# A decoder step on one core: the sample's last sums, square, norm and store laid out as four column quarters on 128 partitions

## The reference

```python
# per token row x of 1024: 8 heads x 16 chosen experts = 128 rows of each table
act = gelu(einsum('chkd,cd->chk', u_emb[eid], xc))
h   = h + einsum('chk,chkd->cd', gate * act, v_emb[eid])
y   = h * rsqrt(mean(h * h, axis=-1) + 1e-6) * g_final
```

## Time and profile before

| | us |
|---|---|
| median of 3 runs | 1046.88 |
| lowest and highest | 1045.89 and 1047.12 |
| span of the profiled execution, first to last instruction | 1044.4 |
| PE, DVE, POOL, ACT busy | 768.4, 761.5, 617.4, 410.3 |
| moved by DMA | 381.40 MB, mean 365 GB/s |

### The profile page before, as it was taken

One profiled execution on the slowest core, in us unless ns is written; L12 is line 12 of the kernel. 1 busy time (PEld: TensorE's weight loads), 2 busy tenths in 40 slices (PEclk: granted clock), 3 DMA queues, 4 the chain that ended last, 5 costly groups with the idle time before them and its releaser, 6 DMA issues.

```text
span 1044.4 us, 13759 instructions
## 1 busy us (share of the span) xinstructions
PE 768.4 (74%) x4077; PEld 379.5 (36%) x4077; DVE 761.5 (73%) x1927; ACT 410.3 (39%) x1159; POOL 617.4 (59%) x584
## 2 busy tenths in 40 slices
PE   8999996456978869777559766765875855645966
PEld 3575872112544546444113333331322422211211
DVE  1362858998877454999977699999554598999441
ACT  1153133223754752333324453732774323324221
POOL 0000257777777776666676757557475665777771
PEclk9999998886987989998767968987687888886899
DMA  9924699999999999999999999999899999999994
GB/s 363 317 106 178 219 331 399 410 404 345 369 397 400 351 410 404 415 407 376 374 375 382 394 406 389 366 392 394 310 407 419 415 415 411 409 402 343 408 410 186
DMA packets 122109, 381.40 MB, mean 365 GB/s; under 512 B 15915, under 2 KB 40315, under 8 KB 116787
## 3 DMA queue, kind: packets, MB, share of 16 engines
q0 software_dynamic: 83696, 304.81, 75.3%
q1 hardware_dynamic: 38338, 75.71, 19.7%
HBM read 378.03 MB, written 4.14 MB: 366 GB/s over the span
## 4 chain that ended last, share of the span: by engine, by line
DVE 43%; PE 21%; DMA 15%; POOL 9%; issue 6%; SPq 3%; ACT 3%; ACTq 0%; DVEq 0%; POOLq 0%
PE bank L445 13%; DVE rows L1388 10%; DMA rows<-in_peer_u,eid 8%; PE acc L445 6%; POOL rows L1883 4%; DVE ql_t L1683 4%; DVE small L1682 4%; DMA w_uq_sb<-in_w_uq 3%; POOL rows L1901 3%; DMA rows<-in_peer_v,eid 2%; DVE more_u L1388 2%; DVE first_u L1388 2%; DVE shared L1714 2%; DVE shared L1725 2%; DMA z<-in_cache_kv 2%
## 5 line engine op out<-in xcount | busy, mean ns | idle before, releaser
L445 PE MATMUL acc<-rows,spread 128*64 128x512 f32 (+1 forms) x1024 | 356.7, 719 | 117.0 <-DMA rows<-in_peer_v,eid 95.2
L1883 POOL DMA_INDIRECT rows<-in_peer_v,eid x256 | 271.2, 1060 | 130.6 <-issue 69.0
L1901 POOL DMA_INDIRECT rows<-in_peer_u,eid x184 | 199.0, 1082 | 99.4 <-issue 48.2
L445 PEld LDWEIGHTS acc<-rows,spread 128*64 128x64 f32 (+1 forms) x1024 | 92.0, 156 | 308.7 <-issue 270.7
L1388 DVE CUSTOM_DVE_ANT_0 rows<-rows,xr_even 128x1024 f32<-128x1024 f32 x89 | 108.3, 1219 | 48.5 <-DMA rows<-in_peer_u,eid 47.6
L1388 DVE CUSTOM_DVE_ANT_0 rows<-rows,xr_odd 128x1024 f32<-128x1024 f32 x95 | 116.1, 1222 | 31.8 <-DMA rows<-in_peer_u,eid 31.1
L1901 POOL DMA_INDIRECT first_u<-in_peer_u,eid x37 | 39.6, 1069 | 96.8 <-DVE eid L1775 79.2
L1056 ACT ACTIVATE spread<-wide_consts,wts 128x64 f32<-128x64 f32 (+1 forms) x288 | 83.7, 337 | 15.5 <-PE acc L445 11.0
L445 PE MATMUL acc<-more_v,spread 128*64 128x512 f32 (+1 forms) x128 | 71.2, 681 | 22.2 <-DMA rows<-in_peer_v,eid 21.3
L1047 ACT ACTIVATE gelus<-dots 128x2 f32<-128x2 f32 x144 | 28.8, 200 | 130.5 <-DVE dots L1388 129.8
L1049 ACT ACTIVATE wts<-gelus,gate 128x1 f32<-128x1 f32 x288 | 69.1, 287 | 4.7
(11 more groups left out here) (267 smaller groups left out, 1336.8 us busy)
## 6 DMA issues: line engine op xcount, KB each, us to landing
wring<-in_w_pq SPq DMA_DIRECT2D x12, 1024.0 KB, 8.0
rows<-in_w_pq SPq DMA_DIRECT2D x3, 2048.0 KB, 8.5
z<-in_w_pq SPq DMA_DIRECT2D x5, 1024.0 KB, 8.0
wring<-in_cache_ckv SPq DMA_DIRECT2D x40, 128.0 KB, 7.0
rows<-in_w_in SPq DMA_DIRECT2D x2, 2048.0 KB, 15.0
rows<-in_peer_v,eid POOLq DMA_INDIRECT x256, 9.6
wring<-in_w_out SPq DMA_DIRECT2D x4, 1024.0 KB, 11.6
wring<-in_cache_kv SPq DMA_DIRECT2D x32, 128.0 KB
```

The costliest lines, as they stand in the source:

```text
L445: return T.matmul(o, lhsT=l, rhs=r, start=start, stop=stop, skip_group_check=True)
L1883: nc.gpsimd.indirect_dma_start(out=v_ring[n % RV], out_offset=None, in_=inp["peer_v"], in_offset=bass.IndirectOffsetOnAxis(ap=eid[t][:, n ...
L1901: nc.gpsimd.indirect_dma_start(out=u_ring[U_PLACE[n]], out_offset=None, in_=inp["peer_u"], in_offset=bass.IndirectOffsetOnAxis(ap=eid[t][: ...
```

## The change

In the sample tile only, the 1024 columns are cut into four quarters of 256, and quarter q stands on partitions 32q to 32q + 31:

- PE: the residual and every sum of the sample tile go to `acc[32q:32q+32, 0:256]`, four matmuls of 256 columns where there were two of 512. The loop over slots is now outside, the one over quarters inside.
- ACT: a root of a constant is taken after the last spread weights, ahead of the wait for the last sums, so that the table is loaded there. The square reads 128x256 and leaves, on each partition, the sum of one quarter.
- PE: a new product with `sel32` (a 128x32 matrix, one where the partition is the token modulo 32) adds the four quarters' sums and puts the total on all four groups of partitions: four matmuls of one column, into a bank of their own. ACT's last root reads it there.
- DVE: reciprocal and norm work on 128 partitions and 256 columns. The gain is needed in the same layout, so SP loads it again in quarters (four loads) after the store of tile 1.
- The store is four transfers of 32 rows of 1 KB, two issued by SP and two by ACT.

```diff
@@ sum_slot
-                    for c in range(2):
+                    for c in range(2 if t < 2 else 0):
                         mm(acc[0:m, c * 512:(c + 1) * 512], ident[0:m, 0:m], x[t][0:m, c * 512:(c + 1) * 512], True, False)
+                    for q in range(0 if t < 2 else 4):
+                        mm(acc[32 * q:32 * q + 32, 0:256], ident[0:32, 0:32], x[t][0:32, 256 * q:256 * q + 256], True, False)
...
+                for j in range(0 if t < 2 else PAIR):
+                    for q in range(4):
+                        i = mm(acc[32 * q:32 * q + 32, 0:256], spread[u % RD][:, j, 0:32],
+                               v_ring[(u * PAIR + j) % RV][:, 256 * q:256 * q + 256], False, False)
@@ end of PE's program
             experts.rest(2)
+            y_square.wait(pe, 2)
+            b = take(pe, ("ysum",))
+            for q in range(4):
+                i = mm(b[32 * q:32 * q + 32, 0:1], sel32, small[:, 12:13])
+            full(i, ("ysum",))
@@ y_root
+                if t == 2:
+                    A.activation(small[:, 14:15], eps, ACT.Sqrt)
                 act.wait_ge(sums_done, (BASE[t] + SLOTS[t]) // PAIR)
...
+                if t == 2:
+                    a = small[:, 12:13]
+                    y_square.send(A.activation(shared[:, 2560:2816], acc[:, 0:256], ACT.Square, accum_out=a), 2)
+                    b = ready(act, ("ysum",))
+                    root_ready.send(A.activation(a, b[:, 0:1], ACT.Sqrt, bias=eps, scale=1.0 / DM), ("y", t))
+                    return
@@ end of ACT's program
             y_root(2)
+            y_ready.wait(act, 2)
+            for q in (2, 3):
+                act.dma_start(out["y_s"][:, 256 * q:256 * q + 256], xn2[32 * q:32 * q + 32, 0:256]).then_inc(y_out, 16)
@@ finish
                 if t == 2:
+                    dve.wait_ge(g_fin_in, 16 * 5)
                     dve.wait_ge(y_out, 32)
-                y_ready.send(norm(acc[0:n, :], g_fin[0:n, :], xn2[0:n, :], 12), t)
+                w = DM if t < 2 else 256
+                y_ready.send(norm(acc[:, 0:w], g_fin[:, 0:w], xn2[:, 0:w], 12), t)
@@ output and the end of SP's program
+                for q in range(0 if t < 2 else 2):
+                    sp.dma_start(out["y_s"][:, 256 * q:256 * q + 256], xn2[32 * q:32 * q + 32, 0:256]).then_inc(y_out, 16)
...
             output(1)
+            for q in range(4):
+                load(g_fin[32 * q:32 * q + 32, 0:256],
+                     bass.AP(inp["g_final"].tensor, inp["g_final"].offset + 256 * q, [[0, 32], [1, 256]]), g_fin_in)
             output(2)
-            sp.wait_ge(y_out, 48)
+            sp.wait_ge(y_out, 16 * 6)
```

More of the change, by code:

```diff
@@ L398, in build @@
         y_ready = Signal("y_ready", tiles)
+        y_square = Signal("square_sums_of_sample_y_ready", [2])
         handovers = {}
@@ L508, in sum_slot @@
                     pe.wait_ge(v_in[v % RV], (v // RV + 1) * 16)
-                for c in range(2):
+                for c in range(2 if t < 2 else 0):
                     for j in range(PAIR):
-                        g, m = (WIDE * j, WIDE) if t < 2 else (0, 32)
+                        g, m = WIDE * j, WIDE
                         i = mm(acc[g:g + m, c * 512:c * 512 + 512], spread[u % RD][:, j, 0:m],
                                v_ring[(u * PAIR + j) % RV][:, c * 512:c * 512 + 512], False, False)
+                for j in range(0 if t < 2 else PAIR):
+                    for q in range(4):
+                        i = mm(acc[32 * q:32 * q + 32, 0:256], spread[u % RD][:, j, 0:32],
+                               v_ring[(u * PAIR + j) % RV][:, 256 * q:256 * q + 256], False, False)
                 i.then_inc(sums_done, 1)
@@ L1437, in finish @@
             def finish(t):
-                n = P[t]
                 root_ready.wait(dve, ("y", t))
-                a = small[0:n, 12:13]
+                a = small[:, 12:13]
                 link(V, V.reciprocal(a, a))
@@ L2009, in output @@
                 y_ready.wait(sp, t)
-                o = out["y_p"][t * 128:(t + 1) * 128, :] if t < 2 else out["y_s"]
-                sp.dma_start(o, xn2[0:P[t], :]).then_inc(y_out, 16)
+                if t < 2:
+                    sp.dma_start(out["y_p"][t * 128:(t + 1) * 128, :], xn2[:, :]).then_inc(y_out, 16)
+                for q in range(0 if t < 2 else 2):
+                    sp.dma_start(out["y_s"][:, 256 * q:256 * q + 256], xn2[32 * q:32 * q + 32, 0:256]).then_inc(y_out, 16)
             load(relb, inp["rel_bias"], hot_in)
```

## The result

| | before | after |
|---|---|---|
| median of 21 runs each, same chip, us | 1044.82 (1041.88 to 1049.67) | 1039.35 (1035.17 to 1045.66) |
| span of the profiled execution, us | 1044.4 | 1035.9 |
| device time of that execution, us | not given | 1037.7 |
| first copy of the sample tokens to the last dot ("stage"), us | 74.84 | 75.77 |
| last dot to the end of the span ("tail"), us | 19.74 | 13.28 |

The ratio is 0.995, with a 95% interval of 0.9937 to 0.9963: 5.2 us faster by the ratio (3.9 to 6.6 by the interval), 5.5 by the medians.

The account below looks back on a forecast made before the run. DMA engines bound the sample tile's expert work; at its end PE's last three pairs, then a serial chain, set the time. Sums 3.3 plus chain 1.8 gave 5.1 us gained, 1046.9 to 1041.8 us, range 1040.0 to 1043.8.

Parts of the forecast that it names:

- the reload: Four loads of the gain, 128 KB, in the DMA-bound stage: cost taken as 0.35 us, bounds nothing and 0.8.
- faster: Whole kernel: time lower by over 0.2%, under 1044.8 us; forecast and two rivals together, chance 0.92.
- The median of the runs is 2.5 above the span; with the same around it, 1046.9 - 5.1 = 1041.8 us: Whole kernel: predicted span of 1039.3 us turned into a run time by keeping the earlier median's distance from the span.
- rival A: Sums at the end: last pair runs at 2.4 GHz, 1.07 us instead of 1.94; 6.2 gained, 1040.7 us; chance 0.33.
- the small product: Chain, PE's product adding the four groups' sums: 0.70 us with the hop, bounds 0.4 and 1.1.
- a landing of 3.4 us: Final store: worst-case landing, as for SP's first transfer in the kernel, giving the store's upper end of 4.2 us.
- PE starts at 1032.6 and ends at 1034.5: Last pair's sums: start after the last rows land at 1032.45; end was 1037.8 before, so 3.3 us gained.
- I take 1.94 us: Sums on PE: a pair falls from 3.59 to 1.94 us at 1.2 GHz; this forecast case had chance 0.50.
- Rival B: Sums: the quarters don't run side by side, a pair stays at 3.6 us, only 1.8 gained, 1045.1 us; chance 0.05.
- It leaves the chain: 1.28 us and a gap, 1.30: Table load on ACT: moves behind the last spread, hidden by PE's last pair, taking 1.30 us off the chain.
- Rivals C and D: Store: C, landing of 3.4 us or somewhat more, 1043.5 us, chance 0.09; D, landing at 9.0 us, 1048.9, chance 0.03.
- either duration fits in: Sums during the DMA-bound stage: pairs of 1.07 or 1.94 us fit within the rows' 5.1 us, so nothing is earned.

Follow-up runs that it names:

- e5: The changed kernel again, nothing altered, on chip B: 1040.17 us against 1043.77 of the kernel before, ratio 0.9962.
- e6: The changed kernel with the loops over slots and quarters swapped in the sums, on chip B: 1039.18 us, ratio 0.9948 to the kernel before.
- e7: The changed kernel without the root of a constant that pulls the table load ahead, on chip B: 1040.3 us, ratio 0.996 to the kernel before.
- e10: The changed kernel with all four sample-tile stores issued by SP, none by ACT, on chip D: a single run of 1095.62 us.
- e8: The changed kernel with PE waiting for each slot's v rows separately and two 64-partition stores instead of four, on chip B: 1041.48 us, ratio 0.9978.

## Why the prediction was right, and where it was not

**The direction and the size.** Forecast 5.1 us gained, measured 5.2 by the ratio and 5.5 by the medians on chip A, and 4.0 by the ratio on chip B: the sum held as far as these can tell. That it held to some tenths is luck. In the traces the clock of the last pair gave 0.86 us more than the forecast's and the stage grew by 0.93 us where the forecast had 0.35 for the reload; the two nearly cancel. The chances gave "faster" 0.92.

**The absolute number.** 1039.35 is 0.65 us below the low end of the range. The step that failed is "The median of the runs is 2.5 above the span; with the same around it, 1046.9 - 5.1 = 1041.8 us", with "runs scatter by half a us". What lies around a span is 1.8 us (1037.7 - 1035.9 here, and 1.8 to 2.0 in nearly all runs that have both numbers); the rest of the 2.5 was scatter between executions, and the three runs lay high. Over 21 runs the kernel before has a median of 1044.82, 0.4 above its profiled span, and the runs spread by 7.8 us. With that base the same sum gives 1044.82 - 5.1 = 1039.7, and rival A's 6.2 gives 1038.6; the measured time is between them. A median of three from such a spread can be off by 2 us, so the range had to be wider by that on both sides. The range's ends are added up wrongly besides. "1040.7 - 0.4 - 0.35 = 1040.2" is 1039.95, and the small product at 0.4 takes only 0.1 more off rival A, which had it at 0.5 already, so the terms give 1040.25; half a us of scatter below either is under 1040.0. At the upper end a landing of 3.4 us gives the 4.2 of the store's own paragraph, not 3.4, and so 1044.3 instead of 1043.5.

**The sums.** "PE starts at 1032.6 and ends at 1034.5" is, counted from the last dot with the forecast's 0.25 us taken into the stage, a start at 7.69 and an end 1.94 us later. Measured: 7.74 and 1.07. So what bounds the end was read rightly, that the last rows' landing gates the last pair and that the others hide, and so was the place of the waits. The clock was half right. "I take 1.94 us" held for all pairs of the stage (0.50 in the windows) and failed for the last one: rival A, with 0.33, is what this execution and e5 did, while e6 and e7 did as the forecast. Gained in the tail ahead of the square: 13.17 - 8.86 = 4.31 us; with the clock as in e7 3.45. A forecast of the clock between these was a coin toss, as the chances 0.50 and 0.33 say. The Trainium skill's rule, in "TensorE: Matmul & The Clock Gate", section "Why this matters for your kernels", that idle gaps send the clock back to half, agrees with the stage; the last pair, after idle times of 1.91, 0.62 and 0.99 us ahead of the last three, shows the way back up, of which no run here gives the condition.

**The order within a pair.** Rival B (quarters that don't run side by side, 1045.1) is excluded by the 1.07 and 1.94 us, and e6 excludes that their order matters.

**The table load.** "It leaves the chain: 1.28 us and a gap, 1.30". It did leave the chain. Taken alone the step is worth only 0.89 us in the changed chain (e7), since the product would hide a third of it. The sum counted the load and the product each in full; against the kernel before that is right, and against the change without this edit it is not. The drain of about 1380 ns that the Trainium skill, "ScalarE: Activation LUTs", section "What ACT_TABLE_LOAD costs", gives beside the load appears neither in the earlier trace rows nor in e7, where 0.02 us lie on either side of it.

**The product over the groups.** Forecast 0.70, bounds 0.4 and 1.1; measured 0.36, below the lower bound (0.41 in e6, where PE runs at 1.2 GHz). The nearest row loaded 128 columns of weights for each record; here eight records take 0.24 us and the rest is two hops. This is the mis-sized term of the chain.

**The store.** Forecast 2.55, measured 1035.9 - 1033.33 = 2.57. Rivals C and D are excluded: ACT's first stores land after 1.7 us. e10 agrees with two queues being worth issue time alone (0.75 measured, 0.8 forecast), as the Trainium skill says in "DMA: Bandwidth & Descriptors", section "Issuing engines are not separate DMA queues".

**The chain.** Forecast 4.78 us from the last sum's end; measured 1035.9 - 1031.43 = 4.47, so 2.1 gained instead of 1.8, nearly all of the difference from the product. From square to end it is 6.55 to 6.63 us in all traces with the old chain and 4.36 to 4.50 in all with the changed kernel's own chain (e7, e8 and e10 alter it), on every chip: the one part of the gain that does not depend on how fast rows come.

**The reload.** "I take 0.35" with bounds of nothing and 0.8. The stage grew by 0.93 us in the one pair of traces. On chips A and B the stages of kernels with the same transfers go from 74.67 to 75.77, and on chip C those with the reload are shorter than those without, so no cost of the reload can be told from scatter; it stays open between nothing and some tenths. The other new part of the stage is the quarter sums, which the forecast put at nothing there ("either duration fits in"). On A and B no run shows a cost of theirs; on C and D the stages with them are 0.3 to 2.2 us longer.

In all: 4.31 (sums, with the lucky clock) + 2.15 (square to end) - 0.93 (stage) = 5.53 us, where the forecast had 3.3 + 1.8.

## What to carry to other kernels

When the transfer engines bound a stage, a faster sum on PE earns nothing in the stage and everything at its end: cost it from the landing of the last rows, not from busy time, and expect it to shrink when those rows come later, as on chips C and D. Widening a serial tail from 32 to 128 partitions pays even with an added product across partitions (0.36 us here), and the saving from the square on is the same on every chip. Take the absolute time from as many runs as there are: a gain of 5 us was forecast to a few tenths, partly by luck, and its time missed by 2.45, of which 2.06 is the median of three.

## What was not expected of the hardware

- **The clock of sparse bursts.** Pairs of 1.93 us, with 3.19 us idle between them, ran at 1.2 GHz through the stage from 975 on. When the last ones came closer (idle 1.91, 0.62, 0.99), the one before the last took 1.51 to 1.54 us and the last 1.07 in two executions, but 1.94 and 1.96 in two others (e7, e6) with idle times of 1.92, 0.62, 0.56 and 1.88, 0.59, 1.36. Timing of the same kind gave either clock.
- **One issue can be slower than two.** Two stores of 64 partitions into two column blocks each moved at 53 GB/s or less and cost 3.0 us more than four stores of 32 partitions (e8).
- **Chips differ.** The kernel before takes 1043.8 to 1044.8 us on two chips, 1092 and 1108 on two others. The transfers reach 409 to 411 GB/s on chip D too; what differs is that the engines stand still there, in waits put down to remote or issue, of which the traces from the first two chips have none. What arrives last, and so what the sums are worth, differs with it.
